# Identity matmuls without a reader in TensorE's waits, at three places of an encoder step

## The reference

```
h = rmsnorm(x) * (1 + sc1) + sh1 ;  proj = h @ w_in        # modulation from silu(c) @ w_ada
y_r = rwkv7_group(proj[:RWKV])        # 8 heads x 64, forward recurrence, token shift
y_g = gla_group(proj[RWKV:])          # 4 heads, key 64 / value 128, chunks
x = x + gt1 * (concat(y_r, y_g) @ w_out)
h = rmsnorm(x) * (1 + sc2) + sh2
x = x + gt2 * hier_moe(h)             # top-1 of 4 groups, top-2 of its 4 SwiGLU experts (width 512)
y = rmsnorm(x) * (1 + scf) + shf
```

## Time and profile before

| what | us |
|---|---|
| median of 3 timed runs | 1585.71 (1585.15 to 1586.64) |
| the profiled execution | 1596.16 |
| its span | 1594.4 |
| TensorE busy in it | 1458.6 (91%) |
| VectorE busy | 531.9 (33%) |
| ScalarE busy | 372.0 (23%) |
| mean granted TensorE clock | 0.945 |

### The profile page before, as it was taken

How to read it: one execution, slowest core, us unless ns; L and a number is a source line. 1 busy time by engine, 2 the same in 40 slices (tenths; PEclk the granted TensorE clock), 3 DMA queues, 4 the chain that set the end, 5 groups by cost and what they waited for, 6 DMA issues and landing times. The chain is left out here.

```text
span 1594.4 us, 28718 instructions
## 1 busy us (share of the span) xinstructions
PE 1458.6 (91%) x12005; PEld 1053.6 (66%) x12005; DVE 531.9 (33%) x993; ACT 372.0 (23%) x766; POOL 173.2 (11%) x298
## 2 busy tenths in 40 slices
PE   4799999999996999999999999965999999999954
PEld 3466666566664877777777767634887878788821
DVE  4244644630211454544444545245000010000028
ACT  5231331311202223224224223110011111111022
POOL 1001112110002102102102102011000000000040
PEclk9899999999997799999999999885999999999977
DMA  8327556532143521321321311026879997988275
GB/s 309 122 92 236 189 182 224 192 110 68 69 126 149 175 54 55 107 60 49 107 66 43 107 35 41 1 60 256 304 252 368 403 382 266 340 330 327 85 278 184
DMA packets 167711, 271.17 MB, mean 170 GB/s; under 512 B 18320, under 2 KB 88846, under 8 KB 167584
## 3 DMA queue, kind: packets, MB, share of 16 engines
q1 hardware_dynamic: 152128, 217.49, 40.3%
q0 software_dynamic: 11920, 38.99, 6.2%
q10 hardware_dynamic: 3536, 12.85, 2.0%
HBM read 215.22 MB, written 54.06 MB: 169 GB/s over the span
## 5 line engine op out<-in xcount | busy, mean ns | idle before, releaser
L2160 PEld LDWEIGHTS banks<-moe_xT,moe_wg 128*128 128x128 f32 x1024 | 132.8, 192 | 9.0 <-issue 9.0
L2160 PE MATMUL banks<-moe_xT,moe_wg 128*128 128x128 f32 (+4 forms) x1024 | 136.8, 292 | 0.8 <-issue 0.8
L2160 PE MATMUL banks<-moe_xT,moe_wu 128*128 128x128 f32 (+4 forms) x1024 | 134.3, 289 | 0.0
L2160 PEld LDWEIGHTS banks<-moe_xT,moe_wu 128*128 128x128 f32 x1024 | 131.2, 191 | 0.0
L653 PE MATMUL banks<-xT,w_v 128*128 128x352 f32 (+1 forms) x384 | 118.7, 469 | 0.0
L653 PE MATMUL banks<-xT,w_r 128*128 128x352 f32 (+1 forms) x384 | 118.6, 469 | 0.0
L653 PE MATMUL banks<-xT,w_k 128*128 128x352 f32 (+1 forms) x384 | 118.3, 468 | 0.0
L1275 PE MATMUL banks<-mixer_w_out,mixer_yT 128*128 128x512 f32 x256 | 117.2, 616 | 0.0
L1548 POOL TENSOR_TENSOR mixer_LTm<-mixer_LT,level 128x256 f32<-128x256 f32 (+1 forms) x90 | 72.2, 825 | 406.9 <-ACT mixer_LTo L1605 278.2
L2189 PE MATMUL banks<-moe_wd,moe_hid 128*128 128x512 f32 x256 | 112.5, 592 | 0.0
L653 PEld LDWEIGHTS banks<-xT,w_v 128*128 128x128 f32 x384 | 72.6, 190 | 45.2 <-issue 2.2
(11 more groups left out here) (456 smaller groups left out, 1958.1 us busy)
## 6 DMA issues: line engine op xcount, KB each, us to landing
moe_wg<-w_expert_gate SPq DMA_DIRECT2D x16, 2048.0 KB
moe_wu<-w_expert_up SPq DMA_DIRECT2D x16, 2048.0 KB, 12.0
moe_wd<-w_expert_down SPq DMA_DIRECT2D x16, 2048.0 KB
feats<-w_ada SPq DMA_DIRECT2D x8, 2048.0 KB, 7.6
wada<-w_ada SPq DMA_DIRECT2D x4, 2048.0 KB, 13.7
feats<-w_ada_final SPq DMA_DIRECT2D x4, 2048.0 KB, 8.1
expert_rows<-moe_yrow ACTq DMA_DIRECT2D x16, 512.0 KB, 6.0
expert_rows<-moe_xTo SPq DMA_DIRECT2D x15, 512.0 KB
```

The costliest lines, as they stand in the source:

```text
L2160: mm = pe.matmul(bank[:, i * n:(i + 1) * n], wt[:, p % 2, q, (t0 + i) * P:(t0 + i + 1) * P], xT[:, p % 2, q, 0:n], start=q == 0, stop=q == ...
```

## The change

A new helper issues `count` matmuls of the identity with itself into the first 128 columns of a bank. Nothing waits for them and nothing reads what they write; TensorE does them in program order, in front of whatever stands behind. It is called seven times:

```diff
+def keep_running(pe, bank, ident, count):
+
+    for _ in range(count):
+        pe.matmul(bank[:, 0:P], ident[:, :], ident[:, :], start=True, stop=True)
@@ recurrence_block, TensorE
             start, swap = first_level(0, 0, P, 1)
+            keep_running(pe, psum[7], ident, 8)
             start()
+            keep_running(pe, psum[7], ident, 6)
             swap()
+            keep_running(pe, psum[7], ident, 8)
             for g in range(2):
                 product(0, 1, g, P)
@@ experts_block, TensorE
+            keep_running(pe, psum[6], ident, 12)
             pe.wait_ge(sg("pads_made"), 3)
             pe.wait_ge(sg("either_made"), 1)
             pe.matmul(psum[0][:, 0:NT * NE], after[:, :], flat(either, PAD), start=True, stop=False)
...
             pe.matmul(psum[0][:, 0:NT * NE], ones[:, :], flat(sum2, PAD - 1), start=False, stop=True).then_inc(sg("ranked"), 1)
 
+            keep_running(pe, psum[6], ident, 52)
             pe.wait_ge(sg("tiles_hot"), 1)
...
             pe.wait_ge(sg("plan_made"), 1)
+            keep_running(pe, psum[6], ident, 20)
             turn_tile(0, 0)
             turn_tile(1, 0)
@@ combine_block, TensorE
             mm.then_inc(sg("shifts_turned"), 1)
+            keep_running(pe, banks[:, 3072:3584], ident, 26)
             for n, m in TILES:
```

## The result

The change made the kernel slower: 1594.36 us against 1587.00 (medians of 20 runs each), a ratio of 1.005 with a 95% interval of 1.0034 to 1.0066. The forecast was 1575.9, from 1570.5 to 1583.0, with a chance of 0.08 for slower. A second timing of the same kernel in another batch gave 1.003 (1.001 to 1.005).

What follows compares the result with a forecast made beforehand. TensorE was taken as the bound between dips of its clock, so earlier stages carry on. Head 2.3, routing 4.9 and last stage 2.6 sum to 9.8 us saved: 1585.71 to 1575.9 us, range 1570.5 to 1583.0.

Steps and rivals of the forecast that it cites:

- the last stage's: Last stage: the 26 raise the clock, the first tile is summed sooner and VectorE follows; 2.6 us saved, ends 0 and 4.3.
- VectorE's unnamed wait: Last stage, 1.7 us without a named releaser: if its end is fixed, it takes the 2.6 away; otherwise it may vanish.
- Head of the recurrence, 2.3 us: First scores 0.5 us and first step's products 1.8 us sooner at the raised clock; ends -0.9 and 3.1.
- TensorE at 9 in every slice: Recurrence: TensorE's busy row read as 9 throughout, so the head's 2.3 us gain would be passed on.
- The slow stretch that the prediction left outside the sum: First chunk, 545 to 558.6 us: 13.6 us of dense work at 0.50; all fast, it would be 6.8 us shorter.
- Routing, 4.9 us: Around plan and experts' start: 3.5 - 0.7 - 0.3 + 0.9 + 1.5 us saved; ends 2.5 and 6.3.
- The plan: Routing: its 36 small matmuls take 7.86 us slow, 3.9 fast; 3.7 us saved, ends 2.5 and 3.9, 3.5 with lateness.
- 0.7 for the gather and 0.3 for the 20: Routing losses: gathers issued sooner meet full DMA engines, 0.7 us; the 20 behind the plan may end late, 0.3 us.
- The experts' start: Behind the routing: second tile's transposes save 0.9 us, first gate products 1.5 us, at the higher clock.
- Identity matmuls don't raise the clock: Rival, all three places: added matmuls all run slow and cost 16.0 us, giving 1601.7 us; chance 8%.
- Part of it lost: Rival: clock falls back at head and plan, last stage's gain mostly taken; 3.6 us saved, 1582.1 us; chance 17%.
- No change: Rival: loads with fixed landing times set the starts, gains waited away; about 1 us saved, 1584.7 us; chance 4%.

Runs made afterwards that it cites:

- before: The kernel without the change, no identity matmuls added; median 1587.00 us in the first timing.
- before_again: The unchanged kernel once more, for a second profile; 1581.9 us.
- all_but_last: The changed kernel without the last stage's 26 matmuls, so head and routing only; ratio 0.9991 to the unchanged kernel.
- head_only: The unchanged kernel with only the 8, 6 and 8 matmuls at the head of the recurrence; ratio 1.0017.
- routing_only: The unchanged kernel with only the routing's 12, 52 and 20 matmuls; ratio 0.9978.
- routing13: The unchanged kernel with only the routing's matmuls, 12, 52 and 13 instead of 20 behind the plan; ratio 0.9981.
- last26: The unchanged kernel with only the last stage's 26 identity matmuls; ratio 1.0013.
- last_wide7: The unchanged kernel with only 7 matmuls of 512 columns in the last stage, in place of the 26 narrow ones; ratio 0.9995.
- after_wide7: The changed kernel with 7 matmuls of 512 columns in the last stage instead of 26 of 128; ratio 0.998, 1583.65 us.
- wide7_13: The changed kernel with 7 wide matmuls instead of 26 in the last stage and 13 instead of 20 behind the plan; ratio 0.9988.
- no_routing: The changed kernel without the routing's 12, 52 and 20 matmuls; ratio 0.9994 to the unchanged kernel.
- after_last24: The changed kernel with 24 instead of 26 identity matmuls in the last stage; ratio 1.0015 to the unchanged kernel.
- last26_front106: The unchanged kernel with the last stage's 26, and all 106 matmuls of head and routing moved to the head's first place; ratio 1.0094.
- no_head_wide7_13: The unchanged kernel with 12, 52 and 13 matmuls around the routing and 7 wide ones in the last stage, none at the head; ratio 0.9989.
- after_74: The changed kernel with 74 instead of 52 identity matmuls in front of the plan; ratio 0.9994 to the unchanged kernel.
- after_last13: The changed kernel with 13 instead of 26 identity matmuls in the last stage; ratio 0.9984 to the unchanged kernel.
- no_head: The changed kernel without the head's 8, 6 and 8 matmuls; ratio 0.9997 to the unchanged kernel.
- after: The changed kernel with all added matmuls, against the unchanged one; 1594.36 us, ratio 1.0050.
- after_again: The changed kernel timed once more in another batch, against the unchanged one; ratio 1.003, 1594.42 us.
- after_last28: The changed kernel with 28 instead of 26 identity matmuls in the last stage; ratio 1.0066 to the unchanged kernel.

## Why the prediction was wrong

**The step that failed is the last stage's.** The prediction counted 2.6 us saved there with ends 0 and 4.3: TensorE sums the first tile sooner and VectorE follows "with the same latency". It said of VectorE's unnamed wait that it might take the gain away "if its end is fixed in time", or vanish. With the first tile summed in time, VectorE followed 13.6 us later, and the stage took 12 us more than with cover alone. The lower end should have been far below nothing. Over all profiles, start of the last stage to the end:

| what the last stage does | kernels | us, mean (each) |
|---|---|---|
| nothing added there | before, before_again, all_but_last, head_only, routing_only, routing13 | 65.7 (67.4, 65.5, 64.8, 64.8, 67.0, 64.5) |
| cover, and the clock stays up through the first tile | last26, last_wide7, after_wide7, wide7_13, no_routing, after_last24, last26_front106, no_head_wide7_13 | 63.0 (62.3 to 64.1) |
| cover, but the clock is back at 0.50 for 3.4 to 6.9 us in the first tile's sum | after_74, after_last13, no_head | 65.2 (65.0, 65.4, 65.1) |
| cover, and the late signal | after, after_again, after_last28 | 75.1 (75.1, 75.1, 75.0) |

The cover by itself was worth 65.7 - 63.0 = 2.7 us in the profiles, against the 2.6 of the forecast, but that the two agree so well is in part luck. VectorE's first step came 2.0 us sooner (13.0 against 15.0 on average; the 15.8 that the prediction started from is the latest of the six), and the other 0.6 or 0.7 is the wait in front of the third tile, which three of those six have (1.7, 1.6, 1.8) and two of the eight (1.4, 0.6): in most it vanished. The timed runs don't confirm the 2.7: last26 stood at 1.0013 and last_wide7 at 0.9995. What was missing is a further outcome, 12 us worse than the second row. The wait on "remote" in front of the third tile was the one row of the profile of before that pointed to it, and I had read it as a small term.

**Head of the recurrence, 2.3 us:** the steps were right, the assumption that TensorE passes the gain on was wrong. The clock rose between 1.4 us in front of the scores and 4.6 us behind their start in the eleven profiles with the head's 22, and 11.0 to 14.3 us behind it in the eight without (last26_front106 left out of both). With the same code in front of it, then, its moment differs by some 6 us between executions. By the second step's products the gain was there: 11.6 us from the scores against 13.9. By the end of the first chunk's inversion (the first matmuls out of `mixer_LTo`) it was gone: 34.0 us with, 33.5 without. To the end of the recurrence it is 558.4 us on average with (554.3 to 564.0) and 558.0 without (553.4 to 566.0). TensorE in the changed kernel shows where it went:

```profile
522.66 0.71 PE L1232 MATMUL banks<-feats 64*128 64x128 f32 x8
524.74 0.71 PE L1232 MATMUL banks<-feats 64*128 64x128 f32 x8 [1.36 <-issue]
...
529.91 0.49 PE L1232 MATMUL banks<-feats 64*128 64x128 f32 x4
531.25 0.94 PE L1232 MATMUL banks<-feats 64*128 64x128 f32 x12 [0.85 <-issue]
```

It stops in the middle of a group of matmuls, where the program waits for nothing; before, the same line (L1226 there) waits in that stretch on VectorE alone, 0.4 us. All profiles together have 38 such waits of TensorE put to "issue" between the first step's products and 32.5 us behind the scores. All 38 stand at the same three places in TensorE's row of instructions, its records 5314, 5569 and 5825 (weight loads counted), whatever the kernel has added in front, and all end 1.25 to 1.54 us behind the landing of a packet of the instruction queue. They sum to 2.8 us on average in the eleven profiles with the head's matmuls (1.5 to 3.6) and to 0.7 in the eight without (0 to 1.7). So some 2 of the 2.3 us won by the clock were lost again in waits for blocks of instructions. (No run took the fetch away, so this rests on the places and ends of the waits.) The prediction had looked for late loads of the next chunk and not for late instructions, and "TensorE at 9 in every slice" could not show either: a slice is 40 us, and the first and last of the recurrence read 6.

On top lies a spread. The slow stretch that the prediction left outside the sum, at 37 us behind the scores, lasted 14 us in before, 10 in after, 20 in last_wide7 and was absent in last26, no_head, after_last13. Before, last26 and last_wide7 have the same code there and took 562.4, 553.4 and 566.0 us from the scores to the recurrence's end. The stretch is the largest difference between them that I see; that it also makes the 1% by which timed runs of one kernel differ is likely, and not shown.

**Routing, 4.9 us:** half of it came. From the plan's start to the last stage's start:

| kernels | us, mean |
|---|---|
| seven without the routing's matmuls | 436.4 (434.3 to 438.0) |
| nine with 12, 52 and 20 | 434.1 (432.7 to 436.3) |
| three with 12, 52 and 13 | 432.7 (432.5 to 432.9) |

So 2.3 us were saved, and 3.7 with 13. (after_74 is left out: its 74 made the plan 2.9 us late, and from there it is 430.8.) Two terms were mis-sized. The plan was put at 3.7 us saved; in the nine it took 6.0 us on average (4.8 to 7.6) instead of 7.9, so 1.8 saved, below my lower end of 2.5. I had noted that back-to-back work of this kind left the clock at 0.50; the other half is that it doesn't hold 1.00 either. And the transposes began 7.1 us behind the plan on average (6.2 to 7.7), against 5.0 in the seven without and 5.9 with 13: 2.1 us later, where the prediction had 1.0 (0.7 for the gather and 0.3 for the 20, which took 7.03 us in after). The experts' start came as forecast or better: from the first transposes to the first gate products it is 3.3 us instead of 5.0 (0.9 forecast), and these take 5.4 instead of 6.9 (1.5 forecast).

**The rivals.** "Identity matmuls don't raise the clock" (8%) is refuted: windows with nothing but them stand at 1.00. It was the only case on the slower side, and the result came out slower for another reason. "Part of it lost" (17%, 3.6 us saved) lies nearest to the change without the late signal, which gave ratios of 0.998 (after_wide7, 3.2 us) to 1.0015 (after_last24). "No change" (4%) had gains "waited away behind each"; that is what happened at the head, with instructions in place of loads.

**The sum as it came out:** head 0, routing 2.3, last stage 2.7, less 12.1 of the late signal (75.1 - 63.0): 7.1 us slower, 0.45%. Measured 0.3 to 0.5%. The same sum makes after_last24 5.0 us faster (0.997); it was timed at 1.0015 (0.9996 to 1.0035), and that difference stays unexplained.

**What stays open** is what holds the signal back. Shown is: it comes with all parts and 26 or 28 matmuls (three profiles of three); it does not come with 24, with 13, with 7 wide ones, without head, without routing, with 22 more in front of the plan, or with the same 106 all at the head. Two things differ from wide matmuls of the same length: the number of instructions in a few microseconds, and the number of records that they leave. That records of updates are missing in all eight profiles with a late signal, and in no other, fits a store of limited size on the way of the records or of the signals, filled while the gathers keep the DMA engines at a share of 1.03; it would give an edge between 24 and 26 and a creeping TensorE. This is a guess. (The Trainium skill, "NOTIFIC — the notification-queue block", 7.1, describes three behaviours of the block that takes the engines' records when a queue of them is full: the new record is dropped, the oldest is overwritten, or the producer is held back. No run here shows which, if any, was at work.) Against so simple a picture stand last26_front106 and last26, with the same burst, the clock up, no record missing and no delay. It wasn't tried whether the delay would be there in an execution that keeps no record at all. The timed runs can't tell, since each lists a span and a clock of its own and so was recorded as well; the 12 us may be a price of recording.

## What to carry to other kernels

Cover a wait of TensorE with few wide matmuls, not many narrow ones: the clock rose as well, and with all other parts in place seven wide ones were 11 us cheaper than 26 narrow ones. Let the cover end before what it waits for can be there at the lower clock, not at the higher one; a matmul too many is paid in full at the slow price. And an unnamed wait in the profile of before, however short, deserves an end of its own on the slow side of the range; a gain in front of a long stage needs the waits of that stage's first steps read, not its share of busy time. Where TensorE runs many small matmuls at the higher clock, look at the packets of its instruction queue as well as at its loads.

## What the runs showed of the hardware

- Matmuls of an identity with an identity, nearly all zeros, raise the granted clock like others: 0.50 in the first 3.9 us of the last stage, 1.00 in the next 4.2, with nothing but these (and two transposes at the start) in both.

```profile
1515.30:1519.20 3.90, 3.86 (x19) 3.82 (x20) 0.00 (x0) 3.89 (x10) 2.66 (x4) 0.50 0.72 225
1519.20:1523.40 4.20, 4.17 (x37) 3.97 (x36) 0.00 (x0) 3.02 (x11) 3.08 (x4) 1.00 1.03 416
```

- Back-to-back matmuls with 34 columns let the clock fall although TensorE was busy without a gap: 36 of them began at 1.00 and had a mean of 0.61 in after, 0.82 in routing_only. Where in the 36 it falls differs between executions.

```profile
1082.03:1087.00 4.97, 4.97 (x36) 4.84 (x36) 1.59 (x2) 0.00 (x0) 0.00 (x0) 0.82 1.05 411
```

- TensorE's signals of finished work can reach the other engines 10 to 14 us late (first and second tile of after, after_again and after_last28), three signals within 0.2 us, with TensorE slowed to some 0.7 us an instruction before, weight loads counted; GpSimd went on issuing its gathers every 1.24 us to the last of them at 21.8 us. Late signals and missing records of semaphore updates came together in eight profiles of twenty, and neither in the other twelve.
- TensorE can wait for its own instructions: 38 waits of 0.17 to 2.5 us in the first 32.5 us of the recurrence, at three fixed places 255 and 256 records apart, each ending 1.25 to 1.54 us behind the landing of a 16.4 KB packet of the instruction queue.
- A higher mean clock isn't a shorter time: the parts at the head and the routing raised the mean over the run from 0.955 to 0.967 (all_but_last), at a ratio of 0.9991. Much of that is the clock of matmuls nobody reads.
